# Three more feed-forward units with their two parts side by side, and forty-four warming products of 32 columns for eleven of 128

## What is computed

```
h2 = rms_norm(x, norm_ffn_pre[l])
ff = jnp.einsum('bsf,fd->bsd',
                jax.nn.silu(jnp.einsum('bsd,df->bsf', h2, w_gate[l]))
                * jnp.einsum('bsd,df->bsf', h2, w_up[l]), w_down[l])
x = x + rms_norm(ff, norm_ffn_post[l])
```

## Time and profile before

| | |
|---|---|
| median of 3 runs | 804.67 us (804.15 to 805.39) |
| the profiled execution | 804.33 us, span 802.5 us |
| PE busy | 796.5 us, 99% of the span |
| PEld, DVE, ACT, POOL busy | 701.4, 571.6, 464.8, 109.3 us |
| PE on the chain that ended last | 96% |
| HBM read | 141.08 MB |

### The profile page before, as it was taken

How to read it: one execution, slowest core, us unless ns; L and a number is a source line. 1 busy time by engine, 2 the same in 40 slices (tenths; PEclk the granted TensorE clock), 3 DMA queues, 4 the chain that set the end, 5 groups by cost and what they waited for, 6 DMA issues and landing times.

```text
span 802.5 us, 13661 instructions
## 1 busy us (share of the span) xinstructions
PE 796.5 (99%) x5842; PEld 701.4 (87%) x5842; DVE 571.6 (71%) x714; ACT 464.8 (58%) x613; POOL 109.3 (14%) x82
## 2 busy tenths in 40 slices
PE   9999999999999999999999999999999999999998
PEld 7999988778888898888888889988899888888887
DVE  6868996896576587766666688688978865556653
ACT  7679784665534575454454575387786644444442
POOL 0102690662000000000000010111610100000000
PEclk9999999999999999999999999999999999999999
DMA  9745444443653655555645555455323555555541
GB/s 322 297 159 166 154 160 155 158 160 118 209 175 144 221 190 175 203 185 183 210 170 197 204 169 205 167 210 163 137 87 109 203 176 192 208 169 200 202 165 53
DMA packets 37820, 143.03 MB, mean 178 GB/s; under 512 B 9426, under 2 KB 11490, under 8 KB 24320
## 3 DMA queue, kind: packets, MB, share of 16 engines
q1 hardware_dynamic: 36576, 138.69, 49.9%
q0 software_dynamic: 1040, 3.43, 1.2%
q10 hardware_dynamic: 144, 0.04, 0.0%
HBM read 141.08 MB, written 1.06 MB: 177 GB/s over the span
## 4 chain that ended last, share of the span: by engine, by line
PE 96%; DVE 1%; POOL 1%; ACT 1%; DMA 1%; issue 0%; SPq 0%; DVEq 0%; POOLq 0%
PE ps L2399 8%; PE ps L2392 7%; PE ps L2039 6%; PE ps L2291 6%; PE ps L2293 6%; PE ps L2292 6%; PE ps L1971 6%; PE ps L2045 6%; PE ps L2042 6%; PE ps L1972 6%; PE ps L1973 6%; PE ps L2397 4%; PE ps L2394 4%; PE ps L2147 2%; PE ps L2306 1%; PE ps L2305 1%
## 5 line engine op out<-in xcount | busy, mean ns | idle before, releaser
L1184 DVE TENSOR_TENSOR wlo<-raw,whi 128x2048 fp32r<-128x2048 f32 (+2 forms) x128 | 289.5, 2263 | 75.2 <-ACT whi L627 73.8
L627 ACT ACTIVATE whi<-raw 128x2048 fp32r<-128x2048 f32 (+2 forms) x128 | 241.2, 1887 | 104.2 <-DMA raw<-w 104.2
L1971 PE MATMUL ps<-xx,whi 128*128 128x256 f32 x396 | 114.1, 288 | 0.0
L1972 PE MATMUL ps<-xx,whi 128*128 128x256 f32 x396 | 112.1, 283 | 0.0
L1973 PE MATMUL ps<-xx,wlo 128*128 128x256 f32 x396 | 112.1, 283 | 0.0
L2291 PE MATMUL ps<-whi,xx 128*128 128x512 f32 x214 | 83.4, 390 | 0.0
L2292 PE MATMUL ps<-whi,xx 128*128 128x512 f32 x214 | 83.3, 389 | 0.0
L2293 PE MATMUL ps<-wlo,xx 128*128 128x512 f32 x214 | 83.3, 389 | 0.0
L2039 PE MATMUL ps<-whi,xx 128*128 128x512 f32 x208 | 83.1, 400 | 0.0
L2045 PE MATMUL ps<-wlo,xx 128*128 128x512 f32 x208 | 81.2, 390 | 0.0
L2042 PE MATMUL ps<-whi,xx 128*128 128x512 f32 x208 | 81.1, 390 | 0.0
(11 more groups left out here) (331 smaller groups left out, 1372.5 us busy)
## 6 DMA issues: line engine op xcount, KB each, us to landing
raw<-w SPq DMA_DIRECT2D x105, 1024.0 KB, 4.8
raw<-w SPq DMA_DIRECT2D x42, 512.0 KB, 5.0
raw<-w SPq DMA_DIRECT2D x8, 256.0 KB, 5.7
x<-xT SPq DMA_DIRECT2D x4, 256.0 KB, 5.8
work<-bias_scratch POOLq DMA_DIRECT2D x1, 1024.0 KB, 7.8
raw<-w SPq DMA_DIRECT2D x4, 192.0 KB, 3.2
out<-x SPq DMA_DIRECT2D x3, 256.0 KB, 2.4
raw<-w SPq DMA_DIRECT2D x3, 240.0 KB, 3.4
```

The lines of the kernel that those rows point to most:

```text
L627: A(hi, full, ACT.Copy).then_inc(sem("hi_ready"), 1)
L1184: V.tensor_tensor(lo, full, hi.bitcast(F32), ALU.subtract)\
L1971: mm(out, hi, xh[:, tile, :], start=start, stop=False, skip_group_check=skip)
L1972: mm(out, hi, xl[:, tile, :], start=False, stop=False, skip_group_check=skip)
```

## The change

Two things. First, units 44, 45 and 46 are done wide too. Their tiles get banks of their own: 0 and 2 for unit 44, 3 and 4 for 45, 1 and 7 for 46. ACT gets six more low copies, DVE six more additions, and the order of both engines around pairs 0 and 1 is written anew; ACT's table for SiLU is loaded by a small instruction of its own ahead of `bc_copy("n3")`. Second, the 11 warming products of 128 streamed columns become 44 of 32 streamed columns; the loaded operand stays 128 x 128.

```diff
@@ -57,9 +57,10 @@
 OUT_PARTS = ((0, 0, 4, 0), (0, 4, 4, 1), (1, 0, 4, 2), (1, 4, 2, 7), (1, 6, 2, 3))
 
 
-WIDE1 = range(2, PAIRS1)
+WIDE1 = range(1, PAIRS1)
 WIDE2 = range(1, PAIRS2)
 GATE_BANKS, UP_BANKS = (0, 1), (2, 7)
+ENTRY_BANKS = ((0, 2), (3, 4), (1, 7))
 
 
 SHARED = (3, 4, 5)
@@ -164,9 +165,10 @@
 def wide_units():
 
 
-    units = []
+    units = [(U_F1 + 1, ENTRY_BANKS[0])]
     for j in WIDE1:
-        units += [(U_F1 + 3 * j - 1, GATE_BANKS), (U_F1 + 3 * j, UP_BANKS)]
+        gate, up = ENTRY_BANKS[1:3] if j == 1 else (GATE_BANKS, UP_BANKS)
+        units += [(U_F1 + 3 * j - 1, gate), (U_F1 + 3 * j, up)]
     for j in WIDE2:
         units.append((U_F2 + 2 * j - 1, (UP_BANKS, GATE_BANKS)[j % 2]))
     return {u: (i, banks) for i, (u, banks) in enumerate(units)}
@@ -874,24 +876,27 @@
                 A(xh[:, tile:tile + 2, :], hid[slot_h], ACT.Copy).then_inc(sem(hidden_name + "_hi"), 1)
 
             split_hi(U_F1 + RING)
+            low_copy(U_F1 + 1, 0, lows[1])
+            low_copy(U_F1 + 1, 1, lows[1])
             split_hi(U_F1 + 1 + RING)
+            A(warm[:, :], half_s[:, 0:1], ACT.Silu)
             bc_copy("n3")
+            low_copy(U_F1 + 2, 0, lows[0])
             silu_pair(0)
+            low_copy(U_F1 + 2, 1, lows[0])
             hidden_hi(0, "hid", 0, 0)
             for j in range(1, PAIRS1):
                 u = U_F1 + 3 * j - 1
-                wide = j in WIDE1
-                if wide:
+                if j > 1:
                     low_copy(u, 0, lows[0])
                 split_hi(u + RING)
-                if wide:
+                if j > 1:
                     low_copy(u, 1, lows[0])
-                    low_copy(u + 1, 0, lows[1])
+                low_copy(u + 1, 0, lows[1])
                 silu_pair(j)
                 if j < PAIRS1 - 1:
                     split_hi(u + 1 + RING)
-                if wide:
-                    low_copy(u + 1, 1, lows[1])
+                low_copy(u + 1, 1, lows[1])
                 hidden_hi(j, "hid", 2 * (j % 2), j % 2)
                 if j == PAIRS1 - 1:
                     split_hi(u + 1 + RING)
@@ -1511,24 +1516,10 @@
             ahead(U_PLE)
 
 
-            def gate_scaled(j, u, bank):
+            def gate_scaled(u, bank):
 
                 dve.wait_ge(sem("unit_used"), u + 1)
-                if not isinstance(j, int) or j >= 1:
-                    dve.wait_ge(sem("gated"), j)
                 V.tensor_tensor(two(silu), two(ps[bank][:, :]), factors_by_tile(2), ALU.mult).then_inc(sem("gate_r"), 1)
-
...
             def low_added(u, m, out, low):
 
@@ -1541,21 +1532,26 @@
                 dve.wait_ge(sem("gated"), j)
                 count(low_added(u, 0, two(silu), lows[0]))
                 link(low_added(u, 1, two(silu), lows[0]))
+                if j == 1:
+                    hidden_lo(0, 0, "hid", 0)
                 V.tensor_tensor(two(silu), two(silu), factors_by_tile(2), ALU.mult).then_inc(sem("gate_r"), 1)
 
-            def up_wide(j, u, m):
-
-                if m == 0:
-                    dve.wait_ge(sem("silu"), j + 1)
+            def silu_scaled(j):
+
+                dve.wait_ge(sem("silu"), j + 1)
+                if j:
                     dve.wait_ge(sem("hid_y"), j)
-                    V.tensor_tensor(two(gated), two(silu), factors_by_tile(2), ALU.mult).then_inc(sem("gated"), 1)
+                V.tensor_tensor(two(gated), two(silu), factors_by_tile(2), ALU.mult).then_inc(sem("gated"), 1)
+
+            def up_added(u, m):
                 count(low_added(u, m, lows[1], lows[1]))
 
             def hidden_wide(j, slot_h):
 
                 dve.wait_ge(sem("gated"), j + 1)
                 dve.wait_ge(sem("dve_chain"), chained[0])
-                dve.wait_ge(sem("hid_lo"), j)
+                if j:
+                    dve.wait_ge(sem("hid_lo"), j)
                 V.tensor_tensor(hid[slot_h], two(gated), lows[1], ALU.mult).then_inc(sem("hid_y"), 1)
 
             def hidden_lo(j, slot_h, hidden_name, base):
@@ -1565,31 +1561,26 @@
                     .then_inc(sem(hidden_name + "_lo"), 1)
 
             norm_factors("n3", 1)
+            up_added(U_F1 + 1, 0)
+            up_added(U_F1 + 1, 1)
             split_lo(U_F1 + RING)
             dve.wait_ge(sem("norm_bcs"), before("bcs", "n3") + 1)
-            gate_scaled(0, U_F1, U_F1 % RING)
+            gate_scaled(U_F1, U_F1 % RING)
             split_lo(U_F1 + 1 + RING)
-            hidden(0, 0, U_F1 + 1, (U_F1 + 1) % RING)
-            hidden_lo(0, 0, "hid", 0)
+            silu_scaled(0)
+            hidden_wide(0, 0)
             for j in range(1, PAIRS1):
                 u = U_F1 + 3 * j - 1
-                wide = j in WIDE1
-                if wide:
-                    gate_wide(j, u)
-                else:
-                    gate_scaled(j, u, u % RING)
+                gate_wide(j, u)
                 split_lo(u + RING)
-                if wide:
-                    up_wide(j, u + 1, 0)
-                if j < PAIRS1 - 1:
+                silu_scaled(j)
+                up_added(u + 1, 0)
+                if 1 < j < PAIRS1 - 1:
                     split_lo(u + 1 + RING)
-                if wide:
-                    up_wide(j, u + 1, 1)
-                    hidden_wide(j, j % 2)
-                else:
-                    hidden(j, j % 2, u + 1, (u + 1) % RING)
+                up_added(u + 1, 1)
+                hidden_wide(j, j % 2)
                 hidden_lo(j, j % 2, "hid", 0)
-                if j == PAIRS1 - 1:
+                if j in (1, PAIRS1 - 1):
                     split_lo(u + 1 + RING)
                 split_lo(u + 2 + RING)
 
@@ -2120,8 +2111,8 @@
                 used(last)
 
             pe.wait_ge(sem("warm_set"), 2)
-            for n in range(11):
-                mm(ps[6 - n // 4][:, (n % 4) * P:(n % 4 + 1) * P], wtile, wtile, start=True, stop=True)
+            for n in range(44):
+                mm(ps[6 - n // 16][:, 32 * (n % 16):32 * (n % 16) + 32], wtile, wtile[:, 0:32], start=True, stop=True)
             for i in range(8):
                 last = first_products(i)
                 if i in ENDS_UNIT:
@@ -2370,16 +2361,7 @@
             used(ple_part(range(4, PLE_EARLY)))
 
 
...
-            def wide_tiles(u, base, between=None):
+            def wide_tiles(u, base, between=None, low=None):
 
 
                 for m in range(2):
@@ -2390,6 +2372,8 @@
                     if m == 0:
                         for k in range(8):
                             mm(o[:, :], whi[:, u % SLOTS, w(k)], xx[:, base + k, :, :], start=k == 0, stop=False)
+                        if low:
+                            low()
                         for k in range(8):
                             last = mm(o[:, 0:T], wlo[:, u % SLOTS, w(k)], xh[:, base + k, :], start=False, stop=k == 7)
                     else:
@@ -2402,28 +2386,30 @@
                 return last
 
             first_unit(U_F1, 8, "n3")
-            first_parts(U_F1 + 1, 8)
+            pe.wait_ge(sem("hi_ready"), U_F1 + 2)
+            used(wide_tiles(U_F1 + 1, 8, low=lambda: arrived(U_F1 + 1)))
             norm_stats("n3", sq3)
+
+            def factors_read():
+                pe.wait_ge(sem("norm_bcs"), before("bcs", "n3") + 1)
 
             def ffn1_step(j, u):
                 first = j == 1
                 pe.wait_ge(sem("lo_ready"), u + 1)
-                if j in WIDE1:
+                if first:
+                    pe.wait_ge(sem("ple_copy"), PLE_EARLY // 2)
+                else:
                     pe.wait_ge(sem("gate_r"), j)
                     pe.wait_ge(sem("hid_y"), j)
-                    used(wide_tiles(u, 8))
-                else:
-                    used(pair_tiles(u, 8, between=lambda: norm_bc("n3")))
+                used(wide_tiles(u, 8, between=(lambda: norm_bc("n3")) if first else None))
                 pe.wait_ge(sem("lo_ready"), u + 2)
-                if j in WIDE1:
-                    used(wide_tiles(u + 1, 8))
-                else:
+                if first:
                     pe.wait_ge(sem("gate_r"), 1)
-                    used(pair_tiles(u + 1, 8))
+                used(wide_tiles(u + 1, 8, between=factors_read if first else None))
                 pe.wait_ge(sem("lo_ready"), u + 3)
                 pe.wait_ge(sem("hid_lo"), j)
                 if first:
-                    pe.wait_ge(sem("ple_copy"), PLE_EARLY // 2)
+                    pe.wait_ge(sem("gate_r"), 2)
                 for kk in range(2):
                     for b in range(4):
                         last = token_down("ff", (u + 2) % SLOTS, 2 * ((j - 1) % 2), b, kk, first and kk == 0, False)
```

18 lines of the change are left out of this document (removed).

## The result

| | before | after |
|---|---|---|
| median of the runs, us | 804.67 (804.15 to 805.39, 5 runs) | 820.87 (818.85 to 821.21, 5 runs) |
| profiled execution, us; its span | 804.33; 802.5 | 820.55; 818.8 |
| first real product, us | 7.07 | 19.87 |
| steady step of 0.46 us for a pair of real products from, us | 7.07 | 25.13 |
| unit 44 to unit 47, us | 17.91 | 17.41 |

The change makes the kernel slower: ratio 1.020 (1.0189 to 1.0211), +16.2 us. The interval lies far above 1; on which side of 2% the loss falls it leaves open. The forecast was 810.3 us; the time lies 0.87 us beyond the upper end of its range, 820.0.

A forecast was written before the change was run, and what follows sets the result against it. PE, busy 99% of the span, bounds the kernel, so losses reach the end nearly one for one. Units -0.6 plus warming +6.4 made +5.8 on 804.33, 810.1, set at 810.3 us towards the median; range 803.7 to 820.0.

The forecast's parts named there:

- The step that failed: Opening: the clock rises at 6.4 us as under the old warming, so 25 loads take 0.215 us, 63 take 0.112.
- rival C: Opening: clock does not rise while the narrow products run; +14.6 us with the units, 819.1 in all; chance 0.32.
- B: The forecast itself: loads bound the warming, clock rises at 6.4, first real product +6.4 us; 810.3 us; chance 0.42.
- the two signs of being wrong: Warming load steps below 0.1 us, or a wait above 1 us between 285 and 309.
- A: Warming: the load isn't a bound, a narrow product takes 0.055 us; only the units' -0.6 left, 804.0; chance 0.14.
- The load as the bound: Warming: each full-width load sets the step, 0.215 us at 1.2 GHz and 0.112 at 2.4, over 88 loads.
- D: Warming: a load takes the same 0.11 us at both clock levels; +3.1 us, 807.6 in all; chance 0.09.
- C's own sum: Loads end at 20.0, +12.9; real products at the lower level +2.3 at least; units -0.6; +14.6, 819.1 us.
- The units: Feed-forward units 44 to 46 done wide: 0.25 us saved on 44, 0.35 on 45 and 46, together -0.60 us.
- B's own bounds: Clock rise anywhere from 5.7 to 7.04 us makes the start 6.2 to 6.9 late; 809.8 to 812 in all.
- DVE's order: Ahead of unit 47: gate of pair 1 ready 0.2 us before PE wants it; taken as 0, range 0 to 1.0.
- The wait for ACT ahead of the first real product: Opening: PE's 0.9 us wait for ACT's weights falls inside the longer warming and is gone.

The follow-up runs named there:

- +8: Changed kernel with the old eleven wide warming products, two products of 32x32 put ahead of them: 804.9 us, ratio 0.9999 to the kernel before.
- +36: Changed kernel with its warming replaced by ten products of 32x32, then ten of the old wide ones: 804.26 us, ratio 1.0003 to the kernel before.
- the warming alone: Kernel before with only its 11 warming products replaced by the 44 of 32 columns, units untouched: 823.85 us, ratio 1.0232.
- the units alone: Changed kernel with the old eleven warming products of 128 columns, so only units 44 to 46 changed: 807.11 us, ratio 1.0036 to the kernel before.

## Why the prediction was wrong

**The step that failed** is the one on the clock: "If these count the same, it rises where it did; I take 6.4". In the kernel before it rose at 6.58, so that reading was right; in the changed kernel it did not rise until 25.15 us. All 88 loads went at the lower level's 0.2136 us, where I had 25 of them so and 63 at 0.112, and six pairs of real products followed at half pace. That is rival C, at 0.32 the second likeliest. Of the two cases I had set B above C on the ground that PE works without a gap in both; the runs show that this is no evidence. 11 products of 32 or 64 columns, with as long a busy time as the old ones, left the clock down too (+2.35 us); 44 with loads of 32 raised it. The duration of a product's record hardly tells these apart (401 ns with 32 columns, 421 with 64 or 128). Neither of the two signs of being wrong came up, load steps below 0.1 us or a wait above 1 us between 285 and 309: they would have shown A or a late DVE, not C.

**What held, term by term.**
- The load as the bound, 0.215 us at the lower level: 0.2136. Rival A is out, and so is D, for which a load would have to take 0.11 at both levels. The 0.112 at the full level was never called on: where the clock rose inside a warming of 128 by 128 (+8 and +36), the steps fell from 0.213 to 0.112, and a load of 128 with a narrow stream at full level is in no run. The page "TensorE: Matmul & The Clock Gate", section "LDWEIGHTS (loading the stationary operand)", of the Trainium skill puts it at columns / 1.2 ns; at 1.2 GHz the trace has twice that, in four kernels.
- C's own sum: last load ends at 20.0 (first real product at 19.87), +12.9 (+12.79), the real products at the lower level +2.3 at least (+2.49; with the warming alone, whose clock rose earlier, +1.72), units -0.6 (-0.53). It comes to +14.6 (+14.8 by these rows). What C lacked is 1.5 us more: 0.16 up to 280, 0.86 by 515 and 0.44 near 560. So even the right case, given alone, would have stopped short at 819.1, and with C's tail in the range its upper end was drawn too tight by as much.
- The units: -0.60 forecast, -0.53 in this kernel, and between -0.52 and -0.55 in all nine kernels that have them, against -0.01 in the two that have not. It is the surest number of the case, and the smallest. The medians can't tell it from nothing (ratios 0.9999 and 1.0003 for the two kernels with wide units and a good opening).
- B's own bounds were worked out a little high: a rise at 5.7 or 7.04 makes the start 6.1 or 6.7 us late, not 6.2 or 6.9. Nothing hangs on it.
- DVE's order: no wait of PE ahead of unit 47, as forecast; it was ready 1.03 us early where I had 0.2.
- The wait for ACT ahead of the first real product is gone, as forecast, and costs nothing to have lost.

**What no case had.** The later waits: with PE 15 us late at the start, transfers, ACT and DVE meet in another order, and at 422 us one of them, behind a transfer that ACT waited 4.00 us for, reached PE as 0.6 (0.83 in the starts behind it). That the transfer is the cause is read from the order of the rows; no run tested it. Waits of 0.3 to 0.6 us between 341 and 423 are in all four kernels with 44 warming products and in none of the others. That they come from the 88 passes rather than from the late start follows from two of them that start on time, but by which way is open. And the break in the rope keys: neither kernel of the comparison has it, so it isn't in the 16.2 us, but the units alone would have made the kernel 0.36% slower by it, which no rival of mine allowed for.

## To carry to other kernels

Filler work that is to raise the clock has to be judged by the pace of the real products behind it, not by its busy time. If the streamed operand is cut, cut the loaded one with it (88 passes took 4.76 us and did the job with loads of 32, 18.98 us and did not with loads of 128). When a change of a few instructions moves the time by 2 to 5 us in a place that it doesn't touch, look for an "issue" wait inside a burst of narrow products and count the instructions ahead of it; a few cheap ones more (here 4 passes, 8 instructions, worth 3 us in the time) may move the burst off the piece's end. A gain of 0.5 us is to be read at the stretch itself, where it repeated within 0.03 us, and not at the median.

## What the hardware showed unexpectedly

- Float32 passes at 1.2 GHz: 0.213 us with a load of 128 columns and 32, 64 or 128 streamed, 0.213 also with a load of 32 and 128 streamed, 0.053 with loads and streams of 32. At 2.4 GHz: 0.112 with both of 128, 0.109 with a load of 32 and 128 streamed, 0.031 with both of 32.
- PE worked without a gap from 1.07 to 25.1 us at the 1.2 GHz level. The Trainium skill, "TensorE: Matmul & The Clock Gate", "Part 1: The HAM clock gate", ties the rise to a time of work and says that it is not a matter of how many products; the changed kernel, the warming alone and the two kernels with 11 products of 32 or 64 columns show that the kind of work counts as well.
- After a wait of 2.55 us in the rope keys the granted clock was 0.57 over the window from 521 to 525; after one of 2.02 us, in the kernel without warming, it was 1.00 over the same window.
- The granted clock of the windows reads 1.00 in the opening at either pace, and 0.57 near 521 us: ahead of the clock's first entry in the trace only the steps tell.
